# A limit of three on the cache-tile loads under way in a hybrid decoder step on one core

## What is computed

```python
qs, kn, vn = att_qkv(rmsnorm(ys, norm_mix[l]), w_in_att[i], q_norm_g[i], k_norm_g[i])
kall = jnp.concatenate([cache_k[i], kn], axis=1)
vall = jnp.concatenate([cache_v[i], vn], axis=1)
res = [dilated_gather(qs, kall, vall, d, w // d) for (w, d) in ((128, 1), (512, 4), (2048, 16))]
os_ = combine_patterns([r[0] for r in res], [r[1] for r in res])
```

## Time and profile before

| | us |
|---|---|
| median of three runs | 2758.44 |
| the profiled execution | 2754.26 |
| its span, first to last instruction | 2752.5 |
| TensorE busy in the span | 2684.9 (98%) |
| VectorE, ScalarE busy | 1739.7 (63%), 946.1 (34%) |
| all DMAs | 259.24 MB, mean 94 GB/s |

### The profile page before, as it was taken

One profiled execution on the slowest core, in us unless ns is written; L12 is line 12 of the kernel. 1 busy time (PEld: TensorE's weight loads), 2 busy tenths in 40 slices (PEclk: granted clock), 3 DMA queues, 4 the chain that ended last, 5 costly groups with the idle time before them and its releaser, 6 DMA issues.

```text
span 2752.5 us, 55925 instructions
## 1 busy us (share of the span) xinstructions
PE 2684.9 (98%) x24161; PEld 2578.0 (94%) x24161; DVE 1739.7 (63%) x2826; ACT 946.1 (34%) x1710; POOL 125.1 (5%) x272
## 2 busy tenths in 40 slices
PE   7999999999999999999999999999999999999998
PEld 7998999999999999999998677777999999999998
DVE  5754537777767776765521665666377777666776
ACT  5543523322222222332223555555232222222222
POOL 1010000000000000000041111110000000000000
PEclk9999999999999999999999999999999999999999
DMA  5030130011111111143255988984101111111112
GB/s 202 32 86 5 61 112 32 32 47 47 56 53 47 47 47 47 47 144 95 82 182 173 279 257 276 308 241 153 46 17 47 47 47 47 47 47 48 60 47 81
DMA packets 145411, 259.24 MB, mean 94 GB/s; under 512 B 10193, under 2 KB 112037, under 8 KB 144656
## 3 DMA queue, kind: packets, MB, share of 16 engines
q1 hardware_dynamic: 129840, 189.26, 22.2%
q0 software_dynamic: 14016, 61.88, 6.8%
q10 hardware_dynamic: 1312, 4.52, 0.5%
HBM read 227.60 MB, written 28.02 MB: 93 GB/s over the span
## 4 chain that ended last, share of the span: by engine, by line
PE 88%; DVE 5%; ACT 3%; DMA 2%; POOL 1%; issue 1%; ACTq 0%; SPq 0%; DVEq 0%; POOLq 0%
PE psum L1575 30%; PE psum L1630 18%; PE psum L484 12%; PE psum L225 11%; PE psum L1550 3%; PE psum L2598 2%; PE psum L2547 2%; PE psum L2507 2%; PE psum L2619 1%; PE psum L2532 1%; DVE smp_kt_blocks L2729 1%; PE psum L2561 1%; ACT att_scores L2688 1%; DVE att_scores L2792 1%; DMA out_v_sample<-qkv_tok 1%
## 5 line engine op out<-in xcount | busy, mean ns | idle before, releaser
L1811 DVE TENSOR_TENSOR x_res<-x_res,psum 128x544 f32<-128x544 f32 x352 | 250.5, 719 | 155.2 <-PE psum L1630 155.2
L484 PE MATMUL psum<-w_hi,h_hi 128*128 128x256 f32 x1096 | 311.5, 284 | 1.0 <-ACT qkv_tok L2093 1.0
L484 PE MATMUL psum<-w_hi,h_lo 128*128 128x256 f32 x1096 | 307.9, 281 | 0.0
L484 PE MATMUL psum<-w_lo,h_hi 128*128 128x256 f32 x1096 | 307.3, 280 | 0.0
L1630 PE MATMUL psum<-ffn_hi,ffn_unit_hi 128*128 128x272 f32 x1408 | 292.6, 289 | 1.8 <-DVE x_res L1811 1.5
L1630 PE MATMUL psum<-ffn_lo,ffn_unit_hi 128*128 128x272 f32 x1408 | 291.5, 288 | 0.0
L1630 PE MATMUL psum<-ffn_hi,ffn_unit_lo 128*128 128x272 f32 x1408 | 290.7, 288 | 0.0
L1575 PE MATMUL psum<-h_hi,ffn_unit_lo 128*128 128x272 f32 x1280 | 265.2, 288 | 0.0
L1575 PE MATMUL psum<-h_lo,ffn_unit_hi 128*128 128x272 f32 x1280 | 264.8, 288 | 0.0
L1575 PE MATMUL psum<-h_hi,ffn_unit_hi 128*128 128x272 f32 x1280 | 264.5, 288 | 0.0
L1630 PEld LDWEIGHTS psum<-ffn_hi,ffn_unit_hi 128*128 128x128 f32 x1408 | 220.7, 188 | 3.1 <-DVE x_res L1811 3.1
(11 more groups left out here) (404 smaller groups left out, 5279.1 us busy)
## 6 DMA issues: line engine op xcount, KB each, us to landing
cache_tile<-in_cache_v SPq DMA_DIRECT2D x64, 512.0 KB, 13.5
cache_tile<-in_cache_k SPq DMA_DIRECT2D x192, 128.0 KB, 5.6
w_raw<-in_w_ffn_gate SPq DMA_DIRECT2D x22, 1024.0 KB, 5.1
w_raw<-in_w_ffn_up SPq DMA_DIRECT2D x22, 1024.0 KB, 5.1
w_raw<-in_w_ffn_down SPq DMA_DIRECT2D x22, 1024.0 KB, 4.8
cache_tile<-in_cache_k SPq DMA_DIRECT2D x32, 512.0 KB, 8.3
w_raw<-in_w_in_att SPq DMA_DIRECT2D x12, 1024.0 KB, 7.1
w_raw<-in_w_in_rec SPq DMA_DIRECT2D x10, 1024.0 KB, 5.0
```

What stands on the lines that cost most here:

```text
L484: mm = pe.matmul(PS[0:n, bank, 0:BW], st[:, k, w:w + n], mv[slot][:, k * BW:(k + 1) * BW], start=(k == 0 and x == 0) if used is None else ...
L1811: dve.tensor_tensor(x, x, pset(dset(g, i)), ALU.add).then_inc(s_res, 1)
```

## The change

Ahead of the load of tile j (j from 3 on), and behind the wait for its buffer, SP also waits until tile j-3 has landed. With it no more than three cache tiles are under way at any time. Nothing else is changed, neither the order of loads nor a buffer.

```diff
@@ -2458,6 +2458,8 @@
                     sp.wait_ge(t_in[bank], count)
                 else:
                     sp.wait_ge(b_vu, 10 * bo + uo - 9)
+            if j >= 3:
+                sp.wait_ge(b_tile[BUF[j - 3]], load_due(j - 3))
             if u < 10 and by_dve(b):
                 for x in range(4):
                     rows = sk[:, b, t, :, 256 * x:256 * x + 256] if t < 8 else sk[:, b, t:16:2, 3, 256 * x:256 * x + 256]
```

## The result

| | before | after |
|---|---|---|
| time, median of 7 runs each (us) | 2758.44 (2756.67 to 2763.41) | 2770.17 (2765.35 to 2772.01) |
| ratio after / before, 95% interval | | 1.0036 (1.0027 to 1.0046) |
| profiled execution: span (us) | 2752.5 | 2763.6 |
| cached value tile, 512 KB, issue to landing (us) | 13.5 | 5.4 |
| TensorE's waits for cache tiles, 1500 to 1930 us | 0.2 | 8.3 |

The change makes the kernel slower by 0.36%, some 10 us by the ratio. The two profiled executions took 2754.26 and 2765.35 us, each 4 to 5 us less than the median of its kernel, and differ by as much as the medians do.

A forecast was written before the change was run, and what follows sets the result against it. It took the DMA engines as saturated in odd attention stretches, with 9.41 us of TensorE "issue" stalls read as late code. -2.2 + 0.2 = -2.0 us took 2758.44 to 2756.4 us, range 2751.0 to 2761.5.

The forecast's parts named there:

- With three always under way the pace is a third of one tile's latency plus 0.1 us: Cache loads in the attention stage: (3.6 + 0.1) / 3 = 1.23 us per 512 KB value tile, 1.74 us per key tile.
- What would show it: Signs for lines 2467 and 2470: landing time 4 to 7 us, unchanged tile use, stalls near 1657, 1686 and 1860 us gone.
- the landings should stay where they are to within a microsecond: Cache tiles under the limit: only the time from issue to landing shrinks; landing times hold within a microsecond.
- the +0.2 us put down for lateness: Tile 19 of sequence 3, the tightest found, slack 0.2 to 0.5 us: +0.2 us, ends 0 and +4 us.
- Nothing of theirs moves: GpSimd's loads are on their own queue, so the limit on SP's loads moves none of them; no cost counted.
- in the crowd: Eight value tiles landing from 1650.6 to 1661.7 us, before the change: 1.59 us apart, the pace set by shared DMA engines.
- the fourth rival: Value tiles of sequences 3 and 5 starve if spaced over 1.59 us: 7.6 us lost, 2766.0 us in all; chance 0.10.
- with GpSimd's loads in the same engines: Mechanism for starving value trains: single latency grows beside GpSimd's loads, so three under way no longer fill the queue.
- the three pieces that were to go: TensorE "issue" stalls behind value trains at 1657.73 (1.01), 1685.69 (0.62) and 1859.45 (0.58): together 2.21 us given back.
- Only three to five are ahead: Stalls of 3.03, 2.46, 1.17 and 0.54 us at quartered key tiles: few tiles queued, so no gain counted.
- the rival that nothing comes back: Code-block delay depends on full DMA engines, not queue length, so all stalls stay: 2758.6 us; chance 0.24.
- the starving rival: Value trains of sequences 3 and 5 come too slowly, TensorE waits over 1 us at line 2619: 2766.0 us; chance 0.10.

## Why the prediction was wrong

**The step that failed** is "With three always under way the pace is a third of one tile's latency plus 0.1 us": (3.6 + 0.1) / 3 = 1.23 us. The formula was sound and the latency put into it was not. With three under way a tile takes 5.1 us on empty engines, and (5.1 + 0.1) / 3 = 1.73, near the measured 1.65. A latency read from tiles that travel alone was carried to tiles that share the way. The prediction had the better number itself: under "What would show it" it expects 4 to 7 us to landing with the limit, and by its own formula that is 1.37 to 2.37 us a tile. So "the landings should stay where they are to within a microsecond" failed with it: from tile 10 to tile 19 the trains of sequences 1, 3 and 5 took 4.8, 2.8 and 4.0 us longer than before, and the +0.2 us put down for lateness became 8.1 us of waiting and 6.8 us of lower clock. "Nothing of theirs moves", said of GpSimd's loads, left out what those loads do to a late train: without the bias load nothing is lost.

**The other side of that comparison**, 1.59 us a tile "in the crowd", was about right as an average. Uninterrupted, tiles 10 to 15 of sequence 3 landed at 1650.9, 1652.3, 1653.6, 1654.9, 1656.1 and 1657.4, 1.30 us apart, and alone the engines do 1.275. Over tiles 10 to 17 the trains of sequences 1, 3 and 5 landed 1.54, 1.54 and 1.53 us apart before and 1.70, 2.40 and 1.74 after (2.40 with the bias load in it). So the point of decision of the fourth rival, trains that starve with a spacing over 1.59 us, was passed in all three. Its place was right (sequences 3 and 5, and also 1). Its 7.6 us of lateness are near the 2.1 + 3.6 + 2.3 us that TensorE waited there, but by luck in part: it had 3.8 us in each of two sequences. Its total of 2766.0 us lacks the price of the clock (+6.8) and the stalls that went (-4.3). Its mechanism, "with GpSimd's loads in the same engines", was half right: the pace falls without them, the loss needs the bias load.

**What a late tile costs** was counted once, as waiting. The clock wasn't foreseen, though the trace of before could have warned. Its two largest "issue" stalls, 3.03 us to 1548.87 and 2.46 us to 1750.06, are each followed by 3.4 us at half clock:

```profile
1550.50:1553.80 3.30, 3.30 (x32) 2.90 (x34) 2.21 (x7) 2.42 (x6) 0.29 (x1) 0.50 1.04 411
1751.90:1755.20 3.30, 3.30 (x38) 2.88 (x40) 1.97 (x7) 2.31 (x7) 0.29 (x1) 0.50 1.04 411
```

**The stalls** gave back 4.3 us where 2.2 were predicted. Of the three pieces that were to go (2.21 us) one of 0.55 us is left, near 1659; the rest of the gain lies elsewhere. The piece of 3.03 us near 1546, which was to stay, shrank to 1.51 us at the same place; the one of 2.46 near 1748 stayed and is 3.01 us after:

```profile
1555.17 0.75 PE L2538 MATMUL psum<-ident,att_q 128*128 128x128 f32 x5 [1.51 <-issue]
```

```profile
1757.21 0.38 PE L2563 MATMUL psum<-smp_kt_blocks,smp_q_blocks 128*32 128x128 f32 x2 [3.01 <-issue]
```

The choice between them rested on a misreading. "Only three to five are ahead" holds for neither: by the landing times nine tiles were under way when each of the two stalls began, and the second still comes with three. The direction was right, and the profiles speak against the rival that nothing comes back: 9.3 to 12.1 us in the seven kernels that don't limit the odd sequences' values to three, 5.8 to 7.3 in the four that do, none with two.

The prediction drew from the Trainium skill, DMA: Bandwidth & Descriptors, section "Queues, rings and completion order", that a code block would wait for one packet however many tiles are queued. These sums don't agree with that, as far as the stalls are code.

That they are code was an inference from the earlier trace rows. The records of the DMA packets bear it out: all 90 "issue" stalls over 0.15 us between 1500 and 1900 us, in the kernel before and ten changed ones, end 1.2 to 1.8 us after a 16.4 KB packet of the instruction queue q8 has been moved, while these packets come only every 8 us. Before, such packets end at 1547.52 and 1748.77 us, and the two largest stalls at 1548.87 and 1750.06. The packets themselves take 0.9 to 1.5 us with and without the limit, so what differs is when they start; why, no run shows.

**What held:** SP's 157 waits cost nothing, and the key tiles kept their pace (keys alone: 0.9996). The time to landing fell from 13.5 to 5.4 us. Tile 19 of sequence 3 was the tightest. The output projection starts 11.0 us later, at 1910.0 instead of 1899.0 us, and takes as long as before from there, 853.6 against 853.5 us: the whole difference is made in the stage. The predicted mark of the starving rival, TensorE waiting over 1 us for a tile at line 2619, is what the profile of the changed kernel shows.

No kernel here beats the kernel before by what a measurement can tell. The gain of up to 4.3 us and the loss sit in the same loads: four or five under way lose nothing and give back nothing, and three without sequences 1, 3 and 5 likewise.

## What to carry to other kernels

A limit on loads under way must be set from a measured train with that limit, not from the latency of a load that travels alone: here 3.5 us alone became 5.1 us with three, and the full pace needed four of 512 KB. Then look at which other loads fall on the last tiles of a train: here the loss needed one of 644 KB. And when waits of TensorE of one to three microseconds are added in some number, price them at about twice their length (here 8.1 us of waits brought 6.8 us of lower clock, and with two under way 20.0 us brought 18.8), because of the half-clock stretch that can follow. For a single wait that is not certain, as the last section shows.

## What the runs showed that was not expected

- 512 KB loads on otherwise empty DMA engines land 3.54, 2.17, 1.65, 1.29 and 1.275 us apart with 1, 2, 3, 4 and 5 under way. The Trainium skill, DMA: Bandwidth & Descriptors, section "Anatomy of one DMA — SWDGE (gpsimd) path", gives about 2.0 us plus the bytes at 436 GB/s for one DMA issued by GpSimd. These loads are issued by SP, but the estimate of 3.2 us that follows for 512 KB is near the 3.5 us measured alone. If three under way hid all of the 2.0 us, they would do 1.2 us a tile by the same figures, again an estimate; the runs show 1.65.
- Cutting a 512 KB tile into quarters makes a train slower, 2.00 to 2.23 us a tile, even with 16 tiles under way; SP's issuing of the quarters alone takes 1.85 us of it.
- Holes of 1.4 to 3 us in TensorE's work were often followed by 3.4 or 6.8 us at half clock, whatever had made them, a tile or an "issue" stall. With four under way so was the wait of 2.68 us to 1668.84, with five that of 1.89 us to 1670.45. But as long a hole can pass without it: the wait of 1.59 us to 1567.46 with the limit on values alone, the stalls of 2.76 us to 1548.39 with four under way and of 2.74 us to 1749.22 with sequences 1, 3 and 5 left free, and, with the limit on keys alone, the stall of 3.29 us to 1749.50, behind which the clock stays at 1.00:

```profile
1749.00:1756.00 7.00, 6.50 (x124) 5.64 (x123) 4.38 (x15) 3.46 (x10) 0.30 (x1) 1.00 1.02 389
```

- Every "issue" stall of TensorE in these profiles ends 1.2 to 1.8 us after a 16.4 KB packet of the instruction queue.
